# An fp32 network of two blocks on one core: two weight chunks behind each layer norm computed from the unnormalised residual, and new orders in the attentions

## The chip, the cores and the metric

One core of one Trainium2 chip. The metric is device time in microseconds (us); lower is better. Three runs of the kernel before gave a median of 1497.17 us (1496.08 to 1500.53).

## The reference, cut to what matters

The input is 256 tokens of width 1024, fp32. Two blocks follow one another, two layers each.

```
first block, per layer i:
  mix = s5_mixer(h) (i = 0)  or  stick_breaking_mixer(h) (i = 1: q, k, v = split(h @ w_qkv), 16 heads of 64)
  h = layer_norm(ALPHA * h + mix)                               # norm n = 0, then n = 2
  h = layer_norm(ALPHA * h + (silu(h @ w_g) * (h @ w_u)) @ w_down)   # n = 1, then n = 3
layer_norm(x) = (x - mean) * rsqrt(var + eps) * g + b
second block (the hybrid), per layer l:
  z = rmsnorm(x) @ w_in ;  split z into q_a k_a v_a | q_m k_m v_m o_m | gates
  x += (sigmoid(g_a) * (attention @ w_a) + sigmoid(g_m) * (mlstm @ w_m)) @ w_out
  x += relu(rmsnorm(x) @ w_ff1)**2 @ w_ff2
```

## The kernel before, in words

Activations lie transposed: features on 128 partitions, the T = 256 tokens on the free axis, in KT = 8 tiles (`kt`). Every weight matrix is cut into chunks of 128 x 2048 fp32 (1 MB) in the fixed order of `plan`. A chunk passes through one of RING = 3 slots: SyncE loads it into `raw` (L341 to L364, it waits for the subtraction of the chunk three before), ScalarE rounds it to `w_hi` (L369), VectorE makes `w_lo = raw - w_hi` (L374), TensorE multiplies. A product is three matmuls, hi x hi, hi x lo, lo x hi (L393 to L395), so a chunk is 48 matmuls of 128x128 on 256 columns. The split of the chunk three ahead is issued behind the work on the present chunk (`split_hi`, `split_lo`).

Each engine runs one program in order; the order is written by hand, and semaphores join the engines.

A sum that ends in a norm runs in `resid_tensor`, `resid_scalar`, `resid_vector`. VectorE adds each finished tile to `res`, forms `xn`, the residual less a rough mean, from tile 4 on, and TensorE turns sums and squares into the mean `dm` and the mean square (`layer_norm_tensor`, six fp32 matmuls, L689 to L694). Then `layer_norm_vector`: L907 to L912 make the variance, ScalarE makes `rstd` (L748, L751), and per tile VectorE scales (L890), ScalarE makes `x_hi` (L759; for n = 3 `res` at L754 and `x_hi` at L776), VectorE `x_lo` (L896 or L901); L915 subtracts the mean from two tiles at a time. `gemm_pair` (L403) then multiplies the first two chunks tile by tile as they come: gu0's chunks 0 and 1 behind n = 0, q0 and k0 behind n = 1, gu1's 0 and 1 behind n = 2, kv and qa0 behind n = 3. The SiLU table is loaded at L848 behind the norm.

First attention (`sb_tensor`, `sb_scalar`, `sb_vector`): twelve chunks in `SB_ORDER` and, for each of eight head pairs hp, `scores(hp)` (L997, needs the evicted k chunk, L540), `soft(hp)` on ScalarE (three passes, L1087 to L1093), `penalties(hp)` on VectorE (L1141, L1146), `running_sums(hp)` on TensorE (L1011), `weights(hp)` (L1099), `outputs(hp)` (L1023, needs the evicted v chunk). `chunk(name, 0)` and `(name, 1)` are the halves of a chunk.

Hybrid (`hyb_tensor`, `hyb_scalar`, `hyb_vector`): VectorE evicts each chunk times `rstd` (L2165). `squares_mean` and `last_square` feed `rstd`; `gate_products` (L1807), `keys`, `rows` and `queries` (L2191 to L2198) prepare; then for four pairs p: `scores(p)` (L1856), `maxima(p)`, `probabilities(p)` (ScalarE, L2053), `normalise(p)`, `transposed(p)` (TensorE), `turned(p)` (ScalarE, L2063), `outputs(p)` (L1881).

Of the kernel before, what the change touches and what calls it, by code (L numbers as in the profile page):

```python
# [24 lines left out]
P = 128  # L25
# [111 lines left out]
SB_ORDER = ("q0", "k0", "v0", "q1", "k1", "v1", "q2", "k2", "q3", "k3", "v2", "v3")  # L137
# [105 lines left out]
def stack(nc, w, out):  # L243
# [4 lines left out]
    with ctx:  # L248
# [30 lines left out]
        rstd = sb("rstd", [P, T], "rstd")  # L279
        vec_rows = sb("vec_rows", [108, P], "misc")  # L280
# [102 lines left out]
        def bank_of(g, k):  # L383
            if g.two:
                i = g.run0
                return (1, 2, 0)[i] if i < 3 else i % 2
            return (g.bank0 + k) % RING
# [15 lines left out]
        def gemm_pair(pe, one, two):  # L403

            items = (one, two)
            for g, idx in items:
                weights_split(pe, g.c0 + idx)
            for kt in range(KT):
                pe.wait_ge(xl_done, KT * one[0].x + kt + 1)
                for g, idx in items:  # L410
                    s = (g.c0 + idx) % RING
                    hi, lo = kt8_view(w_hi, s), kt8_view(w_lo, s)
                    for m in range(2):
                        last = three(PS[:, bank_of(g, idx), m * T:(m + 1) * T], hi[:, kt, m, :], lo[:, kt, m, :], x_hi[:, kt, :],
                                     x_lo[:, kt, :], kt == 0 and m == 0, kt == KT - 1)
                    if kt == KT - 1:
                        last.then_inc(chunk_done, 1)

        def gemm_tensor(pe, g, only=None, kts=(0, KT), first=0):
            drained, base = base_of(g)  # L420

            def body(idx, k, turn):
# [50 lines left out]
            chunk_loop(pe, g.n, max(gemm_head(g), first), 0, body, first)  # L473
# [49 lines left out]
        def gemm_scalar(act, g, only=None, part=None):  # L523
# [24 lines left out]
            chunk_loop(act, g.n, 0, 0, body)  # L548
# [15 lines left out]
        def gemm_vector(dve, g, only=None):  # L564
# [39 lines left out]
            chunk_loop(dve, g.n, 0, 0, body)  # L604
# [54 lines left out]
        
# [22 lines left out]
        def last_square(pe, n):
            pe.wait_ge(sq_done, 5 * n + 5)
            nc.tensor.matmul(PS[:, 5, 0:T], C("mean_d"), sqr[:, 1, T:2 * T], start=False, stop=True,
                             skip_group_check=True).then_inc(var_ready, 1)

        def layer_norm_tensor(pe, n):
            pe.wait_ge(centred, 3 * n + 3)
            nc.tensor.matmul(PS[:, 4, 0:T], C("mean_d"), prod[:, T:2 * T], start=True, stop=False, skip_group_check=True)  # L689
            pe.wait_ge(resid_done, KT * n + 7)  # L690
            nc.tensor.matmul(PS[:, 4, 0:T], C("mean_d"), xn[:, 6, :], start=False, stop=False, skip_group_check=True)
            squares_mean(pe, n)
            pe.wait_ge(resid_done, KT * n + 8)
            nc.tensor.matmul(PS[:, 4, 0:T], C("mean_d"), xn[:, 7, :], start=False, stop=True,  # L694
                             skip_group_check=True).then_inc(dm_ready, 1)
            last_square(pe, n)

        def resid_tensor(pe, g, n, first=True):
# [43 lines left out]
        def norm_scale(act, n):  # L742
# [5 lines left out]
            nc.scalar.activation(rstd[:, :], rstd[:, :] if n < 4 else PS[:, 5, 0:T], ACT.Ln, bias=eps).then_inc(act_step, 1)  # L748
# [4 lines left out]
        def normed_tile(act, n, kt):  # L753
            nc.scalar.activation(res[:, kt, :], xn[:, kt, :], ACT.Identity, bias=ln_bias(n, kt)).then_inc(res_normed, 1)  # L754

        def norm_hi(act, n):
            for kt in range(KT):
                act.wait_ge(scaled, KT * n + kt + 1)
                nc.scalar.activation(x_hi[:, kt, :], xn[:, kt, :], ACT.Identity, bias=ln_bias(n, kt)).then_inc(xh_done, 1)  # L759

        def fourth_norm_scalar(act):

            for kt in range(KT):
                act.wait_ge(scaled, KT * 3 + kt + 1)
                normed_tile(act, 3, kt)
                act.wait_ge(res_normed, KT * 3 + kt + 1)
                gained_hi(act, 4, kt)

        def fourth_squares(act):
            for q in range(3):  # L770
                square_pair(act, 4, None, q)
            square_tile(act, 4, None, 6)
            square_tile(act, 4, None, 7)

        def gained_hi(act, n, t):
            nc.scalar.activation(x_hi[:, t, :], res[:, t, :], ACT.Identity, scale=gain(n, t)).then_inc(xh_done, 1)  # L776

        def resid_scalar(act, g, n):
# [6 lines left out]
            if g.half:  # L785
# [14 lines left out]
                return  # L800
            if n < 4 and g.shape == "kt8":
                resid_hi(act, g, 0)
                nc.scalar.preload_act_table_set(LN_EXP)
                resid_hi(act, g, 1)
                square_pair(act, n, g, 0)
                square_pair(act, n, g, 1)
                square_pair(act, n, g, 2)
                resid_hi(act, g, 2)
                square_tile(act, n, g, 6)
            elif n < 4:  # L810
                for idx in range(7):
                    resid_hi(act, g, idx)
                nc.scalar.preload_act_table_set(LN_EXP)
                square_pair(act, n, g, 0)
                square_pair(act, n, g, 1)
                resid_hi(act, g, 7)
                square_pair(act, n, g, 2)
                resid_hi(act, g, 8)
                resid_hi(act, g, 9)
                square_tile(act, n, g, 6)  # L820
            elif n == 6:
# [11 lines left out]
                return  # L833
            else:
                for idx in range(g.n):
                    resid_hi(act, g, idx)
                return
            square_tile(act, n, g, 7)
            norm_scale(act, n)
            if n == 3:  # L840
                fourth_norm_scalar(act)
            else:
                norm_hi(act, n)
            resid_hi(act, g, last)
            if n == 3:
                fourth_squares(act)
            if n in (0, 2):
                nc.scalar.preload_act_table(ACT.Silu)  # L848
            if n < 3:
                for kt in range(KT):  # L850
                    normed_tile(act, n, kt)
# [28 lines left out]

        def add_squares(dve, n, i):
# [7 lines left out]
        def norm_scaled(dve, n, kt):  # L889
            nc.vector.scalar_tensor_tensor(out=xn[:, kt, :], in0=xn[:, kt, :], scalar=gain(n, kt),  # L890
                                           in1=rstd[:, :], op0=ALU.mult, op1=ALU.mult).then_inc(scaled, 1)

        def norm_lo(dve, n, kt):
            dve.wait_ge(scaled, KT * n + kt + 1)
            dve.wait_ge(xh_done, KT * x_index(n) + kt + 1)
            nc.vector.scalar_tensor_tensor(out=x_lo[:, kt, :], in0=xn[:, kt, :], scalar=ln_bias(n, kt),  # L896
                                           in1=x_hi[:, kt, :].bitcast(F32), op0=ALU.add, op1=ALU.subtract).then_inc(xl_done, 1)
# [6 lines left out]
        def layer_norm_vector(dve, n):  # L904
            dm = PS[:, 4, 0:T]
            dve.wait_ge(dm_ready, n + 1)
            nc.vector.tensor_copy(rstd[:, :], dm).then_inc(dve_step, 1)  # L907
            dve.wait_ge(dve_step, v_count.one())
            nc.vector.tensor_tensor(rstd[:, :], rstd[:, :], dm, ALU.mult).then_inc(dve_step, 1)
            dve.wait_ge(dve_step, v_count.one())  # L910
            dve.wait_ge(var_ready, n + 1)
            nc.vector.tensor_tensor(rstd[:, :], PS[:, 5, 0:T], rstd[:, :], ALU.subtract).then_inc(v_done, 1)  # L912

            def centre(q):
                nc.vector.tensor_tensor(xn[:, 2 * q:2 * q + 2, :], xn[:, 2 * q:2 * q + 2, :],  # L915
                                        dm.unsqueeze(1).to_broadcast([P, 2, T]), ALU.subtract).then_inc(dve_step, 1)
                dve.wait_ge(dve_step, v_count.one())

            centre(0)
            dve.wait_ge(rstd_done, n + 1)  # L920
            for kt in range(KT):
# [1605 lines left out]
```

## Time and profile before

| | |
|---|---|
| median of 3 runs | 1497.17 us |
| the profiled execution, its own time | 1498.88 us |
| its span in the trace | 1496.7 us |
| TensorE matmul busy | 1398.1 us, 93% |
| VectorE busy | 938.0 us, 63% |
| ScalarE busy | 676.1 us, 45% |
| mean granted TensorE clock | 0.978 of full |

PE is TensorE's matmuls, PEld its weight loads, DVE VectorE, ACT ScalarE, SP SyncE. A matmul's duration in the trace is longer than the distance to the next, since they overlap: rates are read from starts. Idle time stands in square brackets with what ended it.

### The profile page before, as it was taken

Reading aid. Unit: us, or ns where it says so; the run is one execution under the profiler, and the core shown is the slowest. Engines: PE = TensorE matmul, PEld = TensorE weight load, DVE = VectorE, ACT = ScalarE, POOL = GpSimd, SP = SyncE. Lnnn points to the kernel's source line nnn. Section 1 sums busy time; section 2 is a strip of 40 time slices with the busy share of each in tenths; the row PEclk is TensorE's granted clock in tenths of the full one; section 3 lists DMA queues with packets and bytes.
Section 4 is the critical chain, followed back from the end, with each engine's and each line's share of the span. In section 5 each row is a group of like instructions: output and inputs, shape, how many; then the busy total and the mean of one; then the engine's idle time right before and its main releaser. Section 6 shows DMA issues by size and latency. Waiting matters only on the chain.

```text
span 1496.7 us, 27718 instructions
## 1 busy us (share of the span) xinstructions
PE 1398.1 (93%) x11695; PEld 1354.5 (90%) x11695; DVE 938.0 (63%) x1217; ACT 676.1 (45%) x805; POOL 10.1 (1%) x8
## 2 busy tenths in 40 slices
PE   4859989999899989999898999999999899999998
PEld 4649989999889989999887999999999799999998
DVE  7996676555654575655675568776457566776542
ACT  4745453333464454343454444534344445444332
POOL 0100000000000000000000000000000000000000
PEclk9979999999999999999999999999999999999999
DMA  6087647676343447666343344556764335456661
GB/s 123 4 126 194 191 112 196 173 192 171 122 159 114 132 111 197 179 187 180 113 142 113 113 166 145 193 172 183 192 189 141 114 113 174 159 174 187 183 192 58
DMA packets 340445, 227.49 MB, mean 152 GB/s; under 512 B 21673, under 2 KB 335249, under 8 KB 340129
## 3 DMA queue, kind: packets, MB, share of 16 engines
q1 hardware_dynamic: 340352, 226.14, 52.9%
q8 instruction: 73, 1.20, 0.4%
q14 instruction: 20, 0.16, 0.0%
HBM read 222.70 MB, written 1.05 MB: 149 GB/s over the span
## 4 chain that ended last, share of the span: by engine, by line
PE 76%; DVE 9%; ACT 7%; issue 3%; SPq 3%; DMA 1%; ACTq 0%; DVEq 0%
PE PS L393 24%; PE PS L394 23%; PE PS L395 23%; ACT w_hi L369 4%; DVE w_lo L374 2%; SPq L1289 2%; PE PS L1011 1%; ACT a_prob L2053 1%; DMA x_chunk<-in_x_dram 1%; PE PS L1357 1%; ACT x_group L1454 0%; DMA raw<-in_ssm_w_glu_dram 0%; PE PS L1322 0%; DVE prod L645 0%; DVE hid_lo L649 0%
## 5 line engine op out<-in xcount | busy, mean ns | idle before, releaser
L374 DVE TENSOR_TENSOR w_lo<-raw,w_hi 128x2048 fp32r<-128x2048 f32 x208 | 476.4, 2291 | 242.7 <-ACT w_hi L369 232.9
L393 PE MATMUL PS<-x_hi,w_hi 128*128 128x256 f32 x1952 | 564.7, 289 | 20.5 <-DVE x_lo L896 11.6
L394 PE MATMUL PS<-x_lo,w_hi 128*128 128x256 f32 x1952 | 559.0, 286 | 0.0
L395 PE MATMUL PS<-x_hi,w_lo 128*128 128x256 f32 x1952 | 558.7, 286 | 0.0
L369 ACT ACTIVATE w_hi<-raw 128x2048 fp32r<-128x2048 f32 x208 | 396.6, 1907 | 243.9 <-PE PS L395 243.6
L393 PEld LDWEIGHTS PS<-x_hi,w_hi 128*128 128x128 f32 x1952 | 381.5, 195 | 25.7 <-issue 20.8
L394 PEld LDWEIGHTS PS<-x_lo,w_hi 128*128 128x128 f32 x1952 | 381.4, 195 | 0.1
L395 PEld LDWEIGHTS PS<-x_hi,w_lo 128*128 128x128 f32 x1952 | 381.4, 195 | 0.0
L393 PE MATMUL PS<-hid_hi,w_hi 128*128 128x256 f32 x1248 | 354.7, 284 | 6.6 <-DVE hid_lo L649 6.6
L394 PE MATMUL PS<-hid_lo,w_hi 128*128 128x256 f32 x1248 | 353.1, 283 | 0.0
L395 PE MATMUL PS<-hid_hi,w_lo 128*128 128x256 f32 x1248 | 353.1, 283 | 0.0
L393 PEld LDWEIGHTS PS<-hid_hi,w_hi 128*128 128x128 f32 x1248 | 239.5, 192 | 8.1 <-DVE hid_lo L649 7.4
L394 PEld LDWEIGHTS PS<-hid_lo,w_hi 128*128 128x128 f32 x1248 | 239.5, 192 | 0.1
L395 PEld LDWEIGHTS PS<-hid_hi,w_lo 128*128 128x128 f32 x1248 | 239.5, 192 | 0.0
L532 ACT ACTIVATE gate_sb<-PS 128x256 f32<-128x256 f32 x52 | 19.9, 383 | 164.2 <-PE PS L395 164.1
L574 DVE TENSOR_TENSOR prod<-PS,gate_sb 128x256 f32<-128x256 f32 x52 | 22.0, 424 | 80.9 <-ACT gate_sb L532 80.9
L535 ACT ACTIVATE gate_sb<-gate_sb 128x512 f32<-128x512 f32 x32 | 20.2, 632 | 99.4 <-DVE gate_sb L587 99.4
L618 DVE SCALAR_TENSOR_TENSOR res<-res,PS 128x256 f32<-128x256 f32 x48 | 19.9, 417 | 38.1 <-PE PS L395 37.9
L393 PE MATMUL PS<-w_hi,x_hi 128*128 128x256 f32 x128 | 37.3, 291 | 0.0
L2053 ACT ACTIVATE a_prob<-PS,neg_m,q_inv 128x128 f32<-128x128 f32 (+1 forms) x32 | 15.9, 506 | 46.3 <-DVE mx L2256 46.3
L901 DVE SCALAR_TENSOR_TENSOR x_lo<-res,vec,x_hi 128x256 fp32r<-128x256 f32 x32 | 15.5, 484 | 33.3 <-ACT x_hi L776 33.3
L394 PE MATMUL PS<-w_lo,x_hi 128*128 128x256 f32 x128 | 36.2, 282 | 0.0
(334 smaller groups left out, 1175.0 us busy)
## 6 DMA issues: line engine op xcount, KB each, us to landing
raw<-in_w_ff_dram SPq DMA_DIRECT2D x128, 512.0 KB, 4.6
raw<-in_ffn_w_gu_dram SPq DMA_DIRECT2D x88, 512.0 KB, 5.0
raw<-in_w_in_dram SPq DMA_DIRECT2D x68, 512.0 KB, 4.7
raw<-in_sb_w_qkv_dram SPq DMA_DIRECT2D x24, 512.0 KB, 4.4
raw<-in_ffn_w_down_dram SPq DMA_DIRECT2D x20, 512.0 KB, 5.0
raw<-in_ssm_w_glu_dram SPq DMA_DIRECT2D x16, 512.0 KB, 6.1
raw<-in_w_out_dram SPq DMA_DIRECT2D x16, 512.0 KB, 4.4
raw<-in_ssm_w_out_dram SPq DMA_DIRECT2D x8, 512.0 KB, 4.0
```

What stands on the lines that cost most here:

```text
L369: nc.scalar.activation(w_hi[s][:, :], raw[s][:, :], ACT.Copy).then_inc(hi_done, 1)
L374: nc.vector.tensor_tensor(w_lo[s][:, :], raw[s][:, :], w_hi[s][:, :].bitcast(F32), ALU.subtract).then_inc(lo_done, 1)
L393: nc.tensor.matmul(dst, lhs_hi, r_hi, start=start, stop=False, skip_group_check=True)
L394: nc.tensor.matmul(dst, lhs_hi, r_lo, start=False, stop=False, skip_group_check=True)
L395: return nc.tensor.matmul(dst, lhs_lo, r_hi, start=False, stop=stop, skip_group_check=True)
L532: nc.scalar.activation(gate_sb[:, k, 0:T], PS[:, bank, T:2 * T], g.func).then_inc(sig_done, 1)
L535: nc.scalar.activation(gate_sb[:, k, :], gate_sb[:, k, :], ACT.Square).then_inc(u_done, 1)
L574: nc.vector.tensor_tensor(prod[:, 0:T], PS[:, bank, 0:T], gate_sb[:, k, 0:T], ALU.mult).then_inc(z_done, 1)
L618: nc.vector.scalar_tensor_tensor(out=res[:, t, :], in0=res[:, t, :], scalar=g.alpha, in1=PS[:, tile_bank(g, t), 0:T], op0=ALU.mult, op1=AL ...
L901: nc.vector.scalar_tensor_tensor(out=x_lo[:, t, :], in0=res[:, t, :], scalar=gain(n, t), in1=x_hi[:, t, :].bitcast(F32), op0=ALU.mult, op1 ...
L1289: sp.dma_start(toep[SH * t:SH * t + SH, BQ * b:BQ * b + BQ, SH * t:P], kern[32 * b:32 * b + SH, :, 0:P - SH * t]).then_inc(k_moved, 16)
L2053: nc.scalar.activation(a_prob[p % 2][:, hd, cols], PS[:, 4 + hd, cols], ACT.Exp, bias=neg_m[:, p, hd, blk:blk + 1], scale=q_inv[:, p, hd, ...
```

## The change

Two chunks behind each of the four layer norms (n = 0 to 3) no longer wait for the normalised tiles. ScalarE and VectorE make `raw_hi` and `raw_lo` from `xn * g` while the sum still runs, with two further columns, -g and b, so that each such matmul moves 258 columns. The norm is applied behind the matmul: `early = (product + dm * colsum0) * rstd`, and then the bias, `colsum1`. The norm's own tiles are worked in pairs, the chunks' splits stand between them, and in the residual of shape kt8 (n = 0 and 2) two splits (`resid_lo` of the last two) move behind tile 7. The SiLU table load moves in front of the normed tiles. The third chunk (gu's number 2, q1, qa1) is now the first that waits for normalised tiles. Both attentions get other orders. Core of the diff:

```diff
-SB_ORDER = ("q0", "k0", "v0", "q1", "k1", "v1", "q2", "k2", "q3", "k3", "v2", "v3")
+SB_ORDER = ("q0", "k0", "q1", "k1", "v0", "q2", "k2", "v1", "q3", "k3", "v2", "v3")
+        def early_tensor(pe, n, slot, kts=(0, KT)):
+            for kt in range(*kts):
+                if slot == 0:
+                    pe.wait_ge(raw_lo_done, KT * n + kt + 1)
+                for m in range(2):
+                    last = three(early_banks(slot)[:, m, 0:T + 2], hi[:, kt, m, :], lo[:, kt, m, :], raw_hi[:, kt, :],
+                                 raw_lo[:, kt, :], kt == 0, kt == KT - 1)
# resid_tensor, behind the last block
             if n < 4:
+                early_tensor(pe, n, 0, (0, 4))
                 layer_norm_tensor(pe, n)
+                early_tensor(pe, n, 0, (4, KT))
+                early_tensor(pe, n, 1)
# ScalarE
+        def layer_norm_scalar(act, g, n):
+            resid_hi(act, g, g.n - 1)
+            norm_scale(act, n)
+            if n in (0, 2):
+                nc.scalar.preload_act_table(ACT.Silu)
+            normed_pair(act, n, 0)
+            normed_pair(act, n, 1)
+            early_columns(act, n, 0)      # two small copies of the column sums, then w_hi of the chunk three on
+            normed_pair(act, n, 2)
+            normed_pair(act, n, 3)
+            early_columns(act, n, 1)
+            early_scalar(act, n, 0)       # SiLU of the gate half, or two bias passes into q0 / k0 / kv / qa0
+            early_scalar(act, n, 1)
+        def normed_pair(act, n, q):       # res of two tiles, then x_hi of both
# VectorE, layer_norm_vector behind the variance (raw_tile_lo: one STT of 256 per tile, earlier, in resid_vector)
             centre(0)
             dve.wait_ge(rstd_done, n + 1)
+            scale(0); centre(1); scale(1); low(0); centre(2); scale(2); low(1)
+            split(0)                      # w_lo of the chunk three on
+            centre(3); scale(3); low(2); low(3)
+            split(1)
+            normalised(0)                 # two STT of 256 from PSUM, one product of 512
+            normalised(1)
+            if n in (0, 2): early_gated(dve, n, 0); early_gated(dve, n, 1)
# first attention, TensorE
-            gemm_pair(pe, (G["q0"], 0), (G["k0"], 0)) ; chunk("v0") ; scores(0) ; chunk("q1", 0) ; scores(1)
-            chunk("q1", 1) ; running_sums(0) ; chunk("k1", 0) ; running_sums(1) ; chunk("k1", 1) ; outputs(0)
...
+            chunk("q1") ; scores(0) ; chunk("k1", 0) ; scores(1) ; chunk("k1", 1) ; running_sums(0)
+            chunk("v0", 0) ; running_sums(1) ; chunk("v0", 1) ; outputs(0) ; scores(2) ; chunk("q2", 0)
+            outputs(1) ; scores(3) ; chunk("q2", 1) ; running_sums(2) ; chunk("k2", 0) ; running_sums(3)
+            chunk("k2", 1) ; scores(4) ; chunk("v1", 0) ; scores(5) ; chunk("v1", 1) ; outputs(2)
+            running_sums(4) ; chunk("q3", 0) ; outputs(3) ; running_sums(5) ; chunk("q3", 1) ; chunk("k3")
+            scores(6) ; chunk("v2", 0) ; scores(7) ; chunk("v2", 1) ; outputs(4) ; running_sums(6)
+            chunk("v3", 0) ; outputs(5) ; running_sums(7) ; chunk("v3", 1) ; outputs(6)
...
# first attention, ScalarE
+            chunk("q1") ; soft(0) ; chunk("k1") ; soft(1) ; weights(0) ; chunk("v0") ; weights(1) ; soft(2)
+            chunk("q2") ; soft(3) ; weights(2) ; chunk("k2") ; weights(3) ; soft(4) ; chunk("v1")
...
# hybrid, TensorE
+            if l: chunk("kv") ; squares_mean(pe, 6) ; last_square(pe, 6) ; chunk("qa0")
+            chunk("qa1") ; chunk("oa0")
+            if l == 0: squares_mean(pe, 4) ; last_square(pe, 4)
+            gate_products() ; chunk("oa1", 0)
+            # l = 1: keys, gate_rows, chunk("oa1", 1); l = 0: chunk("oa1", 1), keys, gate_rows
# hybrid, ScalarE
+            if l == 0: fourth_squares(act) ; split("qa1") ; norm_scale(act, 4) ; key_squares()
...
-            split("qm") ; probabilities(1) ; split("km") ; turned(0) ; probabilities(2) ; split("vm0") ; turned(1)
+            split("qm") ; split("km") ; turned(0) ; probabilities(1) ; split("vm0") ; turned(1) ; probabilities(2)
# hybrid, VectorE, l = 0
+                square_sums(dve, 4) ; lo("qa1") ; wait rstd_done, early_set ; rescale("kv") ; rescale("qa0")
+                evict("qa1") ; evict("oa0") ; gate_parts() ; keys() ; lo("oa0")
             rows() ; queries(0) ; evict("oa1") ; queries(1)      # as before; l = 1 moves gate_parts and keys behind lo("oa0")
```

## Rows read from the trace of the kernel before

**Rows 1.** Page, part 4: the chain that ended last, share of the span by engine.
```profile
PE 76%; DVE 9%; ACT 7%; issue 3%; SPq 3%; DMA 1%; ACTq 0%; DVEq 0%
```

**Rows 2.** Waits of PE: us in total, times, longest us.
```profile
PE PS L1881 <- ACT a_probT L2063: 11.8, 6, 2.4
PE PS L393 <- DVE x_lo L896: 11.6, 3, 3.9
...
PE PS L393 <- DVE x_lo L901: 4.3, 1, 4.3
...
PE PS L1023 <- DVE hid_lo L1153: 1.0, 1, 1.0
```

**Rows 3.** Windows: us, busy us (count) by engine, PEclk, DMA share, GB/s.
```profile
240.00:350.00 110.00, 110.00 (x919) 110.00 (x918) 62.62 (x69) 40.73 (x35) 0.00 (x0) 1.00 0.67 182
...
202.00:204.00 2.00, 2.00 (x13) 2.00 (x12) 1.97 (x5) 0.99 (x2) 0.00 (x0) 0.57 0.00 0
...
813.00:814.00 1.00, 1.00 (x12) 0.68 (x14) 1.00 (x1) 0.00 (x0) 0.00 (x0) 1.00 0.00 0
...
825.00:826.00 1.00, 1.00 (x7) 1.00 (x6) 0.93 (x5) 0.99 (x3) 0.00 (x0) 0.50 0.00 0
```

**Rows 4.** Timeline of PE, norm n = 3 and hybrid: start us, us, line.
```profile
729.29 0.59 PE L689 MATMUL PS<-prod,const 128*128 128x256 f32 x2
...
761.08 0.55 PE L393 MATMUL PS<-x_hi,w_hi 128*128 128x256 f32 x1 [3.46 <-DVE w_lo L374]
...
785.31 0.37 PE L1856 MATMUL PS<-qk_rot 64*128 64x128 f32 x1
...
812.90 0.65 PE L1881 MATMUL PS<-a_probT,va_tok 128*64 128x256 f32 x4 [2.41 <-ACT a_probT L2063]
...
823.86 0.65 PE L1881 MATMUL PS<-a_probT,va_tok 128*64 128x256 f32 x4 [2.40 <-ACT a_probT L2063]
```

**Rows 5.** Timeline of PE: first mean of n = 0 and n = 1, first scores.
```profile
189.53 0.59 PE L689 MATMUL PS<-prod,const 128*128 128x256 f32 x2
...
193.40 0.59 PE L684 MATMUL PS<-sqr,const 128*128 128x256 f32 x2
...
391.36 0.59 PE L689 MATMUL PS<-prod,const 128*128 128x256 f32 x2
...
416.92 0.70 PE L997 MATMUL PS<-qkv 64*128 64x256 f32 x4
```

**Rows 6.** Timeline of DVE around norm n = 0.
```profile
188.88 2.29 DVE L374 TENSOR_TENSOR w_lo<-raw,w_hi 128x2048 fp32r<-128x2048 f32 x1 [0.65 <-ACT w_hi L369]
...
197.64 0.68 DVE L915 TENSOR_TENSOR xn<-xn,PS 128x512 f32<-128x512 f32 x1
198.35 0.48 DVE L890 SCALAR_TENSOR_TENSOR xn<-xn,vec,rstd 128x256 f32<-128x256 f32 x1
```

**Rows 7.** Timeline of ACT behind norm n = 0.
```profile
206.61 1.28 ACT L848 ACT_TABLE_LOAD   x1
207.90 3.31 ACT L754 ACTIVATE res<-xn,vec 128x256 f32<-128x256 f32 x8
...
223.75 0.38 ACT L532 ACTIVATE gate_sb<-PS 128x256 f32<-128x256 f32 x1 [3.57 <-PE PS L395]
```

**Rows 8.** Page, part 6: DMA issues, count, KB each, us to landing.
```profile
raw<-in_ffn_w_gu_dram SPq DMA_DIRECT2D x88, 512.0 KB, 5.0
```

**Rows 9.** Timeline of ACT, first attention: an eviction, one pass of `soft`.
```profile
453.94 0.60 ACT L540 ACTIVATE qkv<-PS 128x512 f32<-128x512 f32 x1 [2.12 <-PE PS L395]
...
474.54 0.85 ACT L1090 ACTIVATE sb_soft<-sb_soft 128x768 f32<-128x768 f32 x1
```

**Rows 10.** Timeline of DVE, first attention: first half of `penalties`.
```profile
421.91 0.96 DVE L1141 SCALAR_TENSOR_TENSOR sb_nl<-PS,sb_soft 128x768 f32<-128x768 f32 x1 [0.16 <-ACT sb_soft L1093]
```

**Rows 11.** Timeline of PE, first attention: `running_sums(1)` after its wait.
```profile
431.23 1.03 PE L1011 MATMUL PS<-sb_nl,const 128*128 128x256 f32 x5 [1.45 <-DVE sb_nl L1146]
```

**Rows 12.** Timeline of ACT, hybrid: the pass that `outputs(1)` waits for.
```profile
812.04 0.81 ACT L2063 ACTIVATE a_probT<-PS 128x768 f32<-128x768 f32 x1
```

More of the change, by code:

```diff
@@ L401, in kt8_view, with early_banks @@
             return w[s][:, :].rearrange("p (k m n) -> p k m n", k=8, m=2)
[L403 to L417 removed]
+        def early_banks(slot):
+            return PS[:, 4 + 2 * slot:6 + 2 * slot, :]
+        def early_tensor(pe, n, slot, kts=(0, KT)):
+            g, idx = early_chunks(n)[slot]
+            s = (g.c0 + idx) % RING
+            if kts[0] == 0:
+                weights_split(pe, g.c0 + idx)
+            hi, lo = kt8_view(w_hi, s), kt8_view(w_lo, s)
+            for kt in range(*kts):
+                if slot == 0:
+                    pe.wait_ge(raw_lo_done, KT * n + kt + 1)
+                    if kt == 0:
+                        pe.wait_ge(col_lo_done, 2 * n + 2)
+                for m in range(2):
+                    last = three(early_banks(slot)[:, m, 0:T + 2], hi[:, kt, m, :], lo[:, kt, m, :], raw_hi[:, kt, :],
+                                 raw_lo[:, kt, :], kt == 0, kt == KT - 1)
+            if kts[1] == KT:
+                last.then_inc(chunk_done, 1)
         def gemm_tensor(pe, g, only=None, kts=(0, KT), first=0):
             drained, base = base_of(g)
+            begun_early = g.func is ACT.Silu or g.name in SB_ORDER
             def body(idx, k, turn):
@@ new lines, in early_scalar @@
+        def early_scalar(act, n, slot):
+            g, idx = early_chunks(n)[slot]
+            act.wait_ge(early_done, 2 * n + slot + 1)
+            act.wait_ge(cols_copied, 2 * n + slot + 1)
+            bias = [col_sums[:, 2 * slot + m, 1:2] for m in range(2)]
+            if g.evac == "gated":
+                gate = early[:, slot, T:2 * T]
+                nc.scalar.activation(gate, gate, g.func, bias=bias[1]).then_inc(sig_done, 1)
+                return
+            dst = hyb_tiles(g) if n == 3 else proj(g, 0).rearrange("p (a t) -> p a t", a=2)
+            for m in range(2):
+                ins = nc.scalar.activation(dst[:, m, :], early[:, slot, m * T:(m + 1) * T], ACT.Identity, bias=bias[m],
+                                           scale=g.scale)
+            ins.then_inc(early_set if n == 3 else act_done, 1)
@@ L836, in resid_scalar, with fourth_squares @@
                     resid_hi(act, g, idx)
[L837 to L851, printed above, removed]
+        def fourth_squares(act):
+            for q in range(3):
+                square_pair(act, 4, None, q)
+            square_tile(act, 4, None, 6)
+            square_tile(act, 4, None, 7)
         def shift_sum(dve, n):
@@ L887, in add_squares, with square_sums @@
             dve.wait_ge(sq_added, 3 * n + i + 1)
[L889 to L897, printed above, removed]
+        def square_sums(dve, n, first=0, end=3):
+            for i in range(first, end):
+                add_squares(dve, n, i)
         def gained_lo(dve, n, t):
@@ new lines, in split, with normalised @@
+            def split(slot):
+                e, idx = early_chunks(n)[slot]
+                split_lo(dve, e.c0 + RING, idx, idx)
+            def normalised(slot):
+                e, idx = early_chunks(n)[slot]
+                dve.wait_ge(cols_copied, 2 * n + slot + 1)
+                for m in range(2):
+                    ins = nc.vector.scalar_tensor_tensor(out=early[:, slot, m * T:(m + 1) * T], in0=dm_sb[:, :],
+                                                         scalar=col_sums[:, 2 * slot + m, 0:1],
+                                                         in1=early_banks(slot)[:, m, 0:T], op0=ALU.mult, op1=ALU.add)
+                ins.then_inc(dve_step, 1)
+                dve.wait_ge(dve_step, v_count.one())
+                both = early[:, slot, :].rearrange("p (a t) -> p a t", a=2)
+                nc.vector.tensor_tensor(both, both, twice[1], ALU.mult).then_inc(early_done, 1)
@@ L919, in layer_norm_vector @@
             centre(0)
             dve.wait_ge(rstd_done, n + 1)
-            for kt in range(KT):
-                norm_scaled(dve, n, kt)
-                if n < 3 and kt >= 1:
-                    norm_lo(dve, n, kt - 1)
-                elif kt >= 1:
-                    gained_lo(dve, 4, kt - 1)
-                if kt % 2 and kt < 7:
-                    centre(kt // 2 + 1)
-            if n < 3:
-                norm_lo(dve, n, 7)
-            else:
-                gained_lo(dve, 4, 7)
-        def square_sums(dve, n, first=0, end=3):
-            for i in range(first, end):
-                add_squares(dve, n, i)
+            scale(0)
@@ L938, in resid_vector @@
         def resid_vector(dve, g, n):
             last = g.n - 1
+            held = 2 if g.shape == "kt8" and n < 4 else last
             for idx in range(g.n):
@@ L958, in resid_vector @@
                     if t == 5 and n < 8:
-                        square_sums(dve, n, 0, 1 if g.half else 3)
-                    if t == 7 and g.half:
+                        square_sums(dve, n, 0, 1 if g.half or n < 4 else 3)
+                    if t == 6 and n < 4 or t == 7 and g.half:
                         square_sums(dve, n, 1, 3)
-                if idx < last or n >= 4:
+                if n >= 4 or idx < held:
                     resid_lo(dve, g, idx)
             if n < 4:
-                layer_norm_vector(dve, n)
-                resid_lo(dve, g, last)
-            if n == 3:
-                square_sums(dve, 4)
+                for idx in range(held, g.n):
+                    resid_lo(dve, g, idx)
+                layer_norm_vector(dve, g, n)
         qkv = sb("qkv", [P, 16, T], "hh", 16 * 4 * T)
@@ L2131, in hyb_scalar @@
             nc.scalar.preload_act_table_set(LN_EXP)
-            split("g0")
-            turned(3)
             split("g1")
```

435 lines of the change are left out of this document (275 added, 160 removed).

## The prediction

> **What bounds the kernel now.** I read the chain by engine first: TensorE holds 76% of it [rows 1], against 93% busy in the table ahead, so time is TensorE's stream plus its gaps. Then the list of what TensorE waits for: 15.9 us in front of the first product behind the four layer norms (L393 on `x_lo`) and 11.8 us in front of the hybrid's `outputs` (L1881 on ScalarE's copy) [rows 2]. Then windows, for the rate: in a stretch of plain products 919 matmuls take 110 us, 0.12 us each, so a chunk of 48 is 5.8 us [rows 3]. The windows also show the second price of a gap. Behind it the granted clock is 0.5, 1.2 GHz: a matmul then takes 0.21 us, and it was still at 0.57 in 202 to 204 us, where the products had begun again at 197.9. One such stretch costs 1.4 to 2.4 us (3.3 to 5.6 us long, 15 to 26 matmuls by 0.09). Which gap brings it is not settled by its length: 2.41 us of idle (812.90) left the clock at 1.00, 2.40 us (823.86) were followed by 0.50 [rows 3, 4]. So I price a gap of 2 to 3 us at half a drop, a longer one at a whole drop.
>
> **Method.** For each region I kept a ledger in the new order: an instruction starts when its engine is free and its releaser has ended, with durations from rows. Its zero is the first mean (L689) of the norm in the trace [rows 4, 5]. Times below are from there.
>
> **FFN entries, n = 0 and 2.** TensorE: 24 early matmuls 2.9, six means to 5.5 (L689 is two records in 0.59 with the last one's tail, 0.43 from mean to mean [rows 5]), 24 and 48 early ones to 14.3. These need no normalised tile, so the old idle stretch is gone. What is late next is gu's chunk 2, the first that needs `x_lo`. VectorE [rows 6]: tile 7 and two `raw_lo` (0.48 each) to 2.4, the two held `w_lo` (2.29 each) to 6.8, three variance steps to 8.1; ScalarE's two for `rstd` to 9.1. Then the table load, 1.28 [rows 7], now in the path: 10.4. A pair costs ScalarE 1.5 (two passes of 0.41 pitch and latency 0.1, one of 512 columns 0.6), VectorE 2.0 (three of 0.68). Pairs 0 and 1 are ready at 12.7 and 14.6, in time. Then ScalarE makes a `w_hi` (1.9) and VectorE its `w_lo` (2.3) before pairs 2 and 3, ready at 19.8 and 21.5. TensorE has done half of chunk 2 at 17.2, idles 2.6, later 0.3, and ends chunk 3 at 29.0. In the trace ScalarE sees chunk 3 at 223.75 - 189.53 = 34.2 [rows 5, 7]. That is -5.2; a gap of 2.6 us may drop the clock, 1.2 on average: -4.0 each, -8.0 for both (-5 to -10.4). The two `w_lo` behind tile 7 free their `raw` slots some 6 us later on SyncE's queue; a load lands in 5.0 us [rows 8], by 12, and its `w_hi` starts at 13.6 at the earliest. Nothing else waits in that queue.
>
> At this place a rule speaks against the change. Row: the load starts 0.02 us behind the pass in front and the next pass starts at 207.90, 1.29 us on [rows 7]; no further pause shows. The Trainium skill, ScalarE: Activation LUTs, What ACT_TABLE_LOAD costs, says a switch costs a drain besides, about 2.66 us in all. By that each FFN entry would lose 1.4 us more, by the row nothing. I go by the row.
>
> **First attention, n = 1.** One `w_lo` less and no table load: pairs 2 and 3 at 18.3 and 20.1, q1 multiplied by 21.6 (idle 1.1 and 0.3). The next order is `scores(0)`, which needs k0 evicted. k0's product is ready at 14.3, but VectorE gets to it only behind pair 3 and the `w_lo` of v0 (23.7): two `normalised` of 1.5 to 26.7, ScalarE's bias passes to 27.6. TensorE idles 6.1 us, queued behind it k1, which is ready; `scores(0)` starts at 27.7. Before: 416.92 - 391.36 = 25.6 [rows 5], also with three chunks done. So +2.1, and +1.9 for the clock behind a gap of 6.1.
>
> The new order then puts six users right behind the last half of the chunk they need (outputs(0), (2), (4), (6) on v, scores(4), (6) on k). Each waits for the chunk's eviction: 0.2 to notice, 0.60 for the pass [rows 9], 0.07 on: 0.87, together +5.2. `running_sums(3)` comes 5.1 us behind q2's end, while `soft(3)` now stands behind q2's eviction and split: 0.2 + 0.5 + 1.8 + three passes of 0.85 + 1.65 of `penalties` (L1141, and L1146 with 0.69) = 6.7 [rows 9, 10]: +1.6. `running_sums(1)` has that wait already, 1.45 [rows 11], and gets 0.2 more; `outputs(1)` and `(7)` wait 0.3 and 1.1 for the pair before, and the old 1.0 at L1023 goes [rows 2]. Sum +7.4. Two waits of 1.7 at half a drop of 0.8: +0.8. First attention: 2.1 + 1.9 + 7.4 + 0.8 = +12.2.
>
> **Hybrid, layer 0.** qa1 and oa0 are done at 28.0. The mean of squares now needs five squares of a ScalarE that finished the bias passes at 28.4, and three sums of VectorE: 32.5, idle 4.5 and a drop. `rstd` comes behind a `w_hi` on ScalarE, at 36.0. The old idle of 3.46 at 761.08 [rows 4], also behind `rstd`, goes; it is in the 56.0 below. From there on VectorE is the chain: `w_lo` 37.0, four evictions 39.5, key rotation to 47.3 (waiting for ScalarE's key scale), `w_lo` 49.5, `rows` 52.8, two query rotations of 2.6 with one eviction: `scores(0)` at 58.6. The same ledger over the old order gives 55.1, the trace 785.31 - 729.29 = 56.0, so I take 59.5: +3.5. It follows an idle of 5.3: a drop, +1.5.
> Then the gain: `turned(p)` no longer stands behind `probabilities(p+1)` on ScalarE. It ends 12.6 behind `scores(0)`, `outputs(0)` is due at 14.7. The waits of 1.85, 2.41 and 2.40 go, with the drop behind the third: -8.1. Layer 0: -3.1.
>
> **Hybrid, layer 1.** `gate_products` comes a chunk later, so `scores(0)` waits for the rotations, 1.0. The other three waits of L1881 (11.8 - 6.7 = 5.1 [rows 2]) go, and one drop of 1.5: -5.6.
>
> **Added and unseen.** 384 early matmuls move 258 columns, 0.8% more, 0.3 us; no row shows any width but 256 in this form (bounds below). The column copies and two small products are 0.3 us off the path. DMA traffic is the same.
>
> **Sum** against the profiled execution's 1498.88 (span 1496.7): -8.0 + 12.2 - 3.1 - 5.6 + 0.3 = -4.2, 1494.7. That execution is 1.7 over the median; from the median, **1493.0**.
>
> **Rivals.**
> 1. *The norms' gaps close and the attention absorbs the rest*: `scores(0)` is not stalled for long and evictions don't show. For it: VectorE is 63% busy. Against: both k0's eviction and the pairs stand in one queue with three `w_lo`. Without the 7.4 and half of the 4.0: 1493 - 9.4 = 1483.6. Chance 0.14.
> 2. *Slower: the wait moves instead of going.* In the hybrid, `scores(p+1)` needs `probabilities(p)`. `probabilities(1)` now stands behind `turned(0)`, and my ledger leaves only 0.8 us between its end and `scores(2)`. If ScalarE's chain is over 0.8 us longer than I count, the wait comes back there; if it comes back whole, 13.2 of gain (-8.1 and -5.1) is lost: 1506. It turns the sign from 4.2 of that on. For it: that queue already made the old wait (L2063 starts right at the end of a w_hi [rows 12]). Against: the pieces moved are each measured. Chance 0.14.
> 3. *258 columns are not at 256's rate.* Speaking for it: no row. Against: nothing in the rate of rows 3 depends on the last columns. At half rate 384 x 0.09 = +36: 1529; no change at 0.011 us a matmul. Chance 0.04.
> 4. *The change is even*: every 2.6 us gap drops the clock and the short attention waits do too, +4: 1497. Chance 0.22.
> The forecast keeps 0.46, its own range 1489 to 1496.
>
> **Numbers.** Under 0.3% (4.5 us) this kernel can't be told from no change. Faster by more, under 1492.7: rival 1 and near half of the forecast and a part of rival 4, 0.42. Within: 0.38. Slower, over 1501.7: rivals 2 and 3 and tails, 0.20. The range takes in rival 1 in part and rival 4: 1484 to 1503.
>
> **What would show it.** Right: no idle stretch over 1 us between the residual's end and the third chunk; 2 to 3 us inside chunk 2 of gu; L997 first starting some 27 to 28 us behind the norm's first mean with an idle of 5 to 7 us; six idles near 0.9 us in front of `outputs` and `scores`; no idle in front of `outputs` in the hybrid, and idles of 4 to 5 us at the first mean of squares and at `scores(0)` of hybrid layer 0. Wrong: `scores(0)` of the first attention with under 3 us idle (then rival 1), idles in front of the second hybrid `scores` (rival 2), early matmuls more than 0.13 us apart (rival 3).

## The result, and the profile after

The changed kernel takes 1504.74 us (median of 4 runs, 1502.73 to 1507.06) against 1496.62: ratio 1.005, 95% interval 1.0027 to 1.0074. It is 8.1 us slower, where 4.2 less were forecast.

The chain by engine (page, part 4) gives less to TensorE and more to the two others than in [rows 1]:

```profile
PE 73%; DVE 12%; ACT 10%; issue 3%; SPq 2%; DMA 1%; ACTq 0%; DVEq 0%
```

The waits of TensorE after (us in total, times, longest), to be held against [rows 2]. The wait at the hybrid's `outputs` is gone, as forecast. The first of these rows has nothing of before and nothing in the prediction to answer to it:

```profile
PE PS L705 <- DVE prod L942: 8.8, 2, 4.4
...
PE PS L400 <- DVE x_lo L1025: 7.0, 4, 2.4
...
PE PS L1990 <- DVE qk_rot L2343: 6.3, 2, 5.3
PE PS L1142 <- ACT qkv L847: 5.7, 1, 5.7
...
PE PS L712 <- DVE sqr L988: 3.6, 1, 3.6
PE PS L1156 <- DVE sb_nl L1286: 3.4, 2, 1.7
```

I cut the span at the first mean of each norm. It is L689 before [rows 4, 5] and L723 after; of its starts I take off 2.9 us, since 24 early matmuls now stand in front of it. The two further cuts are the waits of 1.8 us near the end of each hybrid layer (L1920 before, L2054 after, on `hid_lo`). Timeline of TensorE after: the missed wait, the four means, and the waits that were forecast:

```profile
181.64 0.80 PE L705 MATMUL PS<-prod,const 128*128 128x256 f32 x1 [4.39 <-DVE prod L942]
...
196.79 0.60 PE L723 MATMUL PS<-prod,const 128*128 128x256 f32 x2
...
213.40 0.39 PE L400 MATMUL PS<-x_hi,w_hi 128*128 128x256 f32 x1 [2.39 <-DVE x_lo L1025]
...
394.43 0.60 PE L723 MATMUL PS<-prod,const 128*128 128x256 f32 x2
...
419.98 1.22 PE L1142 MATMUL PS<-qkv 64*128 64x256 f32 x4 [5.71 <-ACT qkv L847]
...
549.34 0.60 PE L723 MATMUL PS<-prod,const 128*128 128x256 f32 x2
...
746.83 0.60 PE L723 MATMUL PS<-prod,const 128*128 128x256 f32 x2
...
777.12 0.86 PE L712 MATMUL PS<-sqr,const 128*128 128x256 f32 x2 [3.58 <-DVE sqr L988]
...
803.06 0.58 PE L1990 MATMUL PS<-qk_rot 64*128 64x128 f32 x1 [5.29 <-DVE qk_rot L2343]
```

| stretch, us | before | after | difference | forecast |
|---|---|---|---|---|
| start to the first mean of n = 0 | 189.53 | 193.89 | +4.4 | 0 |
| n = 0 to n = 1 (FFN) | 201.83 | 197.64 | -4.2 | -4.0 |
| n = 1 to n = 2 (first attention and its residual) | 136.11 | 154.91 | +18.8 | +12.2 |
| n = 2 to n = 3 (FFN) | 201.82 | 197.49 | -4.3 | -4.0 |
| n = 3 to the end of hybrid layer 0 | 147.35 | 142.92 | -4.4 | -3.1 |
| to the end of hybrid layer 1 | 371.59 | 365.57 | -6.0 | -5.6 |
| rest | 248.47 | 248.48 | 0 | 0 |

The sum is +4.2, from two single executions; the first row holds 2.6 us of luck in the start-up (TensorE's first GLU matmul at 115.84 against 118.41). From there to the first mean it is 78.05 against 71.12: +6.9. So two rows are off, by 6.9 and 6.6, and each holds one wait at L705.

**What L705 waits for.** It is `shift_mean`, the rough mean of the first four tiles. VectorE's timeline after:

```profile
169.01 0.78 DVE L633 SCALAR_TENSOR_TENSOR res<-res,PS 128x256 f32<-128x256 f32 x2 [0.89 <-PE PS L402]
177.28 0.18 DVE L972 SCALAR_TENSOR_TENSOR raw_lo<-vec,raw_hi 128x8 fp32r<-128x8 f32 x1 [7.49 <-ACT raw_hi L802]
177.37 0.17 DVE L974 TENSOR_TENSOR raw_lo<-vec,raw_hi 128x8 fp32r<-128x8 f32 x1
177.45 2.28 DVE L381 TENSOR_TENSOR w_lo<-raw,w_hi 128x2048 fp32r<-128x2048 f32 x1
179.65 0.74 DVE L633 SCALAR_TENSOR_TENSOR res<-res,PS 128x256 f32<-128x256 f32 x2
180.43 0.69 DVE L940 TENSOR_TENSOR prod<-res 128x512 f32<-128x512 f32 x1
181.16 0.43 DVE L942 TENSOR_TENSOR prod<-prod 128x256 f32<-128x256 f32 x1
```

and ScalarE's, same stretch:

```profile
169.37 1.91 ACT L376 ACTIVATE w_hi<-raw 128x2048 fp32r<-128x2048 f32 x1 [3.58 <-PE PS L402]
171.30 1.28 ACT L893 ACT_TABLE_LOAD   x1
175.13 1.91 ACT L376 ACTIVATE w_hi<-raw 128x2048 fp32r<-128x2048 f32 x1 [2.54 <-PE PS L402]
176.95 0.20 ACT L801 ACTIVATE raw_hi<-vec 128x8 fp32r<-128x8 f32 x1
177.05 0.20 ACT L802 ACTIVATE raw_hi<-vec 128x8 fp32r<-128x8 f32 x1
```

The reader is to see a chain through three queues (a split is numbered here by the chunk of the residual whose slot it takes over). VectorE reaches the low parts of the two further columns (0.18 and 0.17 us) behind tile 1, in chunk 0 of the residual. ScalarE makes their high parts behind `w_hi` number 1, which waits until TensorE has finished chunk 1. VectorE idles 7.49 us, and `w_lo` number 0, tiles 2 and 3 and the sum for L705, none of which needs the columns, stand behind. Before, that `w_lo` waited for nothing but its own `w_hi`, and the sum ended at 179.38, in time for TensorE. VectorE's timeline of the kernel before:

```profile
173.96 2.29 DVE L374 TENSOR_TENSOR w_lo<-raw,w_hi 128x2048 fp32r<-128x2048 f32 x1 [1.52 <-ACT w_hi L369]
...
178.96 0.42 DVE L858 TENSOR_TENSOR prod<-prod 128x256 f32<-128x256 f32 x1
```

In the FFN's residual (n = 1 and 3) the sum runs over ten chunks, the columns come in time and L705 doesn't wait. Behind the 4.39 us TensorE ran at 1.2 GHz (the first of the windows below; the second is behind the 2.39 us, the third is `k1` behind `scores(0)`; columns as in [rows 3], the granted clock behind the five engines):

```profile
182.00:184.00 2.00, 2.00 (x9) 1.82 (x9) 2.00 (x2) 0.00 (x0) 0.00 (x0) 0.50 1.15 324
216.00:218.00 2.00, 2.00 (x13) 2.00 (x12) 1.45 (x1) 0.52 (x1) 0.00 (x0) 0.57 0.24 59
422.00:424.00 2.00, 2.00 (x11) 2.00 (x11) 0.00 (x0) 1.94 (x4) 0.00 (x0) 0.50 0.00 0
```

### The profile page after: what moved, and what is told of

It is laid out like the page before. It is cut to its first block, busy times and chain, and to the rows that moved or that the text cites. A ratio compares the mean times of both kernels' runs of the same rounds, so it can differ in the third digit from the quotient of the medians.

```text
span 1500.9 us, 27760 instructions
## 1 busy us (share of the span) xinstructions
PE 1396.3 (93%) x11695; PEld 1353.0 (90%) x11695; DVE 956.1 (64%) x1255; ACT 689.2 (46%) x853; POOL 10.1 (1%) x8
## 4 chain that ended last, share of the span: by engine, by line
PE 73%; DVE 12%; ACT 10%; issue 3%; SPq 2%; DMA 1%; ACTq 0%; DVEq 0%
PE PS L400 22%; PE PS L401 22%; PE PS L402 22%; DVE w_lo L381 4%; ACT w_hi L376 4%; SPq L1423 1%; PE PS L1156 1%; PE PS L1475 1%; DMA x_chunk<-in_x_dram 1%; ACT res L815 1%; PE PS L1491 1%; ACT terms L1617 1%; DMA raw<-in_ssm_w_glu_dram 0%; ACT x_group L1588 0%; PE PS L1456 0%
## 5 line engine op out<-in xcount | busy, mean ns | idle before, releaser
L400 PE MATMUL PS<-x_hi,w_hi 128*128 128x256 f32 x1824 | 524.6, 288 | 11.3 <-DVE x_lo L1025 7.0
L401 PE MATMUL PS<-x_lo,w_hi 128*128 128x256 f32 x1824 | 519.4, 285 | 0.0
L402 PE MATMUL PS<-x_hi,w_lo 128*128 128x256 f32 x1824 | 519.2, 285 | 0.0
L400 PEld LDWEIGHTS PS<-x_hi,w_hi 128*128 128x128 f32 x1824 | 353.3, 194 | 16.1 <-DVE x_lo L1025 7.8
L401 PEld LDWEIGHTS PS<-x_lo,w_hi 128*128 128x128 f32 x1824 | 353.4, 194 | 0.1
L402 PEld LDWEIGHTS PS<-x_hi,w_lo 128*128 128x128 f32 x1824 | 353.2, 194 | 0.0
L400 PE MATMUL PS<-raw_hi,w_hi 128*128 128x258 f32 x128 | 36.9, 288 | 0.0
L402 PE MATMUL PS<-w_hi,x_lo 128*128 128x256 f32 x128 | 36.1, 282 | 0.0
```

The source lines that it names most:

```text
L400: nc.tensor.matmul(dst, lhs_hi, r_hi, start=start, stop=False, skip_group_check=True)
L401: nc.tensor.matmul(dst, lhs_hi, r_lo, start=False, stop=False, skip_group_check=True)
L402: return nc.tensor.matmul(dst, lhs_lo, r_hi, start=False, stop=stop, skip_group_check=True)
```

## The experiments

All ratios are to the kernel before, run beside them (1496.38 for the first four, 1496.08 for the others).

**e1, the columns earlier.**

```diff
                 for idx in range(begin + 1):
                     resid_hi(act, g, idx)
+                    if idx == (0 if g.shape == "kt8" else 1):
+                        raw_columns_hi(act, g, n)
                     if idx == 0:
                         nc.scalar.preload_act_table_set(LN_EXP)
-                    if idx == 1:
-                        raw_columns_hi(act, g, n)
```

> The changed kernel with one pair of small passes moved: in the residuals of n = 0 and 2 ScalarE makes the two high columns (L801, L802) behind the w_hi of chunk 0 and ahead of the table load, no longer behind the w_hi of chunk 1. Theory (the missed wait): VectorE stood 7.49 us at its low columns for them, and that made TensorE's shift_mean (L705) wait 4.4 us twice, each with a stretch at the low clock of 1.3 to 2.5 us behind it. Without it 2 x (4.4 + 2.0) = 12.8 less than the changed kernel's 1504.7: 1492, and no wait at L705. Rival A: shift_sum is late anyway, since a w_lo and two tiles stand in front of it; then L705 still waits 2 us or more and the time stays at 1498 or above. Rival B: most of the 8 us lies in the first attention, which took 18.8 us more against 12.2 of my ledger; then only about 6 come back, 1498.

Measured: 1492.85, ratio 0.9976 (0.9966 to 0.9987): 11.9 us less than the changed kernel. VectorE's sum is ready in time, and L705 is gone from the list of waits:

```profile
172.73 0.18 DVE L972 SCALAR_TENSOR_TENSOR raw_lo<-vec,raw_hi 128x8 fp32r<-128x8 f32 x1 [1.73 <-ACT raw_hi L802]
172.82 0.17 DVE L974 TENSOR_TENSOR raw_lo<-vec,raw_hi 128x8 fp32r<-128x8 f32 x1
172.91 2.29 DVE L381 TENSOR_TENSOR w_lo<-raw,w_hi 128x2048 fp32r<-128x2048 f32 x1
...
177.53 0.42 DVE L942 TENSOR_TENSOR prod<-prod 128x256 f32<-128x256 f32 x1
```

TensorE's timeline of e1 starts L705 without idle:

```profile
178.30 0.59 PE L705 MATMUL PS<-prod,const 128*128 128x256 f32 x2
```

From the first GLU matmul (117.05) to the first mean it is 71.01 us, as before the change (71.12). n = 1 to n = 2 takes 148.26. Both rivals fall: neither does a wait stay at L705, nor is the first attention's excess over my ledger its own. This one misplaced pair of 0.2 us passes made the change slower; with it mended the change is 3.5 us faster than before (0.24%).

**e2, ScalarE's hybrid order alone, on the kernel before.**

```diff
             split("qm")
-            probabilities(1)
             split("km")
             turned(0)
-            probabilities(2)
+            probabilities(1)
             split("vm0")
             turned(1)
-            probabilities(3)
+            probabilities(2)
             split("vm1")
             turned(2)
+            probabilities(3)
```

> The kernel before with one thing alone: on ScalarE turned(p) goes ahead of probabilities(p+1) in both hybrid layers. Theory: the six waits at outputs (11.8 us) go, with two low-clock stretches of 1.5 behind them (three of the waits were long enough): 1496.6 - 13 = 1483.5, and scores(p+1) doesn't wait. Rival (rival 2 of the prediction): the wait comes back at scores(p+1), which needs probabilities(p); then the waits sum to over 8 us again and the time is over 1491.

Measured: 1483.06, ratio 0.9909 (0.9894 to 0.9925): -13.3. The head of its list of waits, nothing left out; a row for L1881 would stand second, with 11.8:

```profile
PE PS L1394 <- DMA toep<-kern: 11.8, 1, 11.8
PE PS L393 <- DVE x_lo L896: 11.6, 3, 3.9
PE PS L1296 <- DMA tb<-in_ssm_log_dt_dram: 8.0, 1, 8.0
PE PS L393 <- DVE hid_lo L649: 6.6, 4, 1.7
PE PS L1302 <- DMA c_rows<-in_ssm_c_re_dram: 4.5, 1, 4.5
PE PS L393 <- DVE x_lo L901: 4.3, 1, 4.3
```

Layer 0 is 7.0 shorter in the trace, layer 1 6.9. So the part of the change that is worth most is three calls moved in one engine's list, and rival 2 is refuted: `scores(p+1)` doesn't take the wait over. One term is not as the prediction had it. The stretch at the low clock behind layer 0's third wait (0.50 in 825 to 826 us before) was counted among the gains. In this execution the wait is gone and the granted clock is 0.54 in 826 to 828 us all the same, with no idle in front of it.

**e3, e1 with other orders in the first attention.** Chunks in the changed kernel's sequence; TensorE's list begins

```diff
             chunk("q1")
-            scores(0)
             chunk("k1", 0)
-            scores(1)
             chunk("k1", 1)
-            running_sums(0)
+            scores(0)
             chunk("v0", 0)
-            running_sums(1)
             chunk("v0", 1)
-            outputs(0)
-            scores(2)
+            scores(1)
+            running_sums(0)
             chunk("q2", 0)
...
```

and ScalarE's and VectorE's lists follow it; in the same manner each user stands half a chunk or more behind what it needs.

> e1_columns with other orders in the first attention on the three engines: the same chunks in the same sequence, but scores, running sums and outputs stand at least half a chunk behind the eviction and the passes that they need, and scores(0) stands behind k1. Theory (order): the 15 us of waits in this attention and the drop behind the 5.7 us one come from where the users stand; the ledger gives 121.3 us for the stretch against 139.7, so 18.4 less than e1_columns: 1473.5. Rival (work): VectorE and ScalarE are the limit there, and the waits only move; then under 6 us come back, over 1486.

Measured: 1474.05, ratio 0.9860 (0.9845 to 0.9875): 18.8 less than e1. n = 1 to n = 2 takes 129.83, and from `scores(0)` on TensorE has no idle over 0.3 us in the attention. The engines were not the limit; the order was.

**e5, only TensorE's list, and only behind `k1`.**

```diff
             chunk("k1", 1)
-            running_sums(0)
             chunk("v0", 0)
-            running_sums(1)
             chunk("v0", 1)
+            running_sums(0)
+            running_sums(1)
             outputs(0)
             scores(2)
             chunk("q2", 0)
...
```

> e1_columns with only TensorE's list in the first attention changed, and that only behind k1: scores, running sums and outputs 1 to 7 stand half a chunk or more behind the eviction or pass that they need. scores(0), scores(1) and the lists of ScalarE and VectorE are those of the changed kernel. It splits the first attention's price in two. Theory: the eight short waits there (0.7 to 1.7 us each, my +7.4 and +0.8) are the place of the users alone; the ledger gives 129.1 against 139.7, so 10.6 less than e1_columns: 1482.3. What is left to e3_attention (1474.05), 8.2, is the wait of scores(0) for k0's late eviction and the low clock behind it. Rival: with ScalarE and VectorE unchanged the waits only move along TensorE's list; then 1488 or more.

Measured: 1482.08, ratio 0.9904 (0.9887 to 0.9921): 10.8 less than e1. The one idle over 0.3 us left between `scores(0)` and the residual's end is that of `scores(0)` itself:

```profile
413.61 1.23 PE L1142 MATMUL PS<-qkv 64*128 64x256 f32 x4 [4.82 <-ACT qkv L847]
```

So of 18.8 us, 10.8 were users put right behind an eviction or a pass. The other 8.0 (1482.08 - 1474.05) I put down to the entry: `scores(0)` behind VectorE's queue, 4.82, and the low clock behind it (0.50 in 414 to 418 us). That is argued, since e3 also reorders the lists of ScalarE and VectorE; but e5 has no other wait over 0.3 us behind q1 that e3 could remove.

**e4, e3 with other orders behind the norms.**

```diff
# ScalarE
+            early_columns(act, n, 0)
+            normed_pair(act, n, 0) ; (1) ; (2) ; (3)
             if n in (0, 2):
                 nc.scalar.preload_act_table(ACT.Silu)
-            normed_pair(act, n, 0) ; (1) ; early_columns(act, n, 0) ; normed_pair(act, n, 2) ; (3)
             early_columns(act, n, 1)
# VectorE (the last held resid_lo stood ahead of the variance)
-            centre(0) ; rstd ; scale(0) ; centre(1) ; scale(1) ; low(0) ; centre(2) ; scale(2) ; low(1) ; split(0)
-            centre(3) ; scale(3) ; low(2) ; low(3) ; split(1) ; normalised(0) ; normalised(1)
+            centre(0) ; (1) ; (2) ; rstd ; scale(0) ; (1) ; resid_lo(last) ; scale(2) ; low(0) ; centre(3) ; scale(3)
+            low(1) ; (2) ; (3) ; split(0) ; normalised(0) ; normalised(1) ; split(1)
```

> e3_attention with other orders behind the four norms: all four pairs of normed tiles before the second w_hi and before both w_lo of the next chunks, the last held w_lo behind rstd instead of ahead of the variance, the table load behind the pairs, the early chunks' eviction ahead of the second w_lo. Theory: the idle of 2.4 us inside the third chunk and the low clock behind it (1.5) go at n = 0, 2 and 3, and the mean of squares and the first scores of hybrid layer 0 come 3.8 earlier: 2 x 4.3 + 1.6 + 3.8 = 14 less than e3_attention. Rival: the w_lo that is put back is late for the fourth chunk and the idle moves there; then under 5 us less.

Measured: 1463.24, ratio 0.9777 (0.9763 to 0.9791): -10.8 against e3, of the 14 expected. Per stretch the traces show -3.9 and -4.0 at the FFN entries (198.26 to 194.41, 198.07 to 194.09), -2.0 in the attention and -2.2 in hybrid layer 0. The idle inside the third chunk is gone; what is left there is 0.38 and 0.70 us for the fourth chunk's `w_lo`, the rival in small. The first scores of layer 0 start 54.6 us behind the norm's first mean, where e3 has 59.1: 4.5 earlier, for the 3.8 expected. Behind them this execution has two stretches at 1.2 GHz (granted clock 0.54 in 806 to 808 us, 0.50 in 820 to 822), where e3's stands at 1.00, and so only 2.2 of the 4.5 are left at the layer's end. In layer 1, which wasn't touched, it has 3.0 more, in two such stretches again.

**e6, e4 with hybrid layer 0's statistics pulled forward.**

```diff
# ScalarE, n = 3, behind the four pairs (was behind the bias passes of kv and qa0)
+                for q in range(3): square_pair(act, 4, None, q)
+                square_tile(act, 4, None, 6) ; square_tile(act, 4, None, 7)     # behind early_columns(1)
# ScalarE, hybrid: norm_scale(4), which makes rstd, ahead of split("qa1")
# VectorE: square_sums(4) behind split(0); in the hybrid lo("qa1"), lo("oa0") ahead of keys()
# TensorE, layer 0
-            chunk("oa0") ; squares_mean(4) ; last_square(4) ; gate_products() ; chunk("oa1") ; keys() ; gate_rows()
+            chunk("oa0", 0) ; squares_mean(4) ; last_square(4) ; chunk("oa0", 1) ; gate_products()
+            chunk("oa1", 0) ; keys() ; gate_rows() ; chunk("oa1", 1)
```

> e4_norm with hybrid layer 0 changed: ScalarE squares the normed tiles right behind them, ahead of the bias passes of kv and qa0, TensorE takes the mean of squares in the middle of oa0, and rstd comes some 8 us earlier; the key scale and two w_lo are pulled forward with it. Theory: the 2.1 us wait at the mean of squares and 3 of the 5 us at scores(0) were rstd's lateness; the ledger has scores(0) at 49.1 instead of 54.3 behind the norm's first mean: 5.2 less than e4_norm, 1458.0. Rival: VectorE's rotations and rows set scores(0) whatever rstd does; then only the 2.1 come back, 1461.

Measured: 1455.18, ratio 0.9724 (0.9702 to 0.9746): -8.1 against e4, where 5.2 were expected; the traces of both give -5.8 in layer 0 (140.99 to 135.19). In e4 the two waits were 2.06 and 5.01, with one of 1.94 at `row_columns` between them, which e6 no longer has. Timelines of e4, `rstd` and the first scores:

```profile
737.92 0.42 ACT L790 ACTIVATE rstd<-rstd 128x256 f32<-128x256 f32 x1
...
760.91 0.58 PE L1992 MATMUL PS<-qk_rot 64*128 64x128 f32 x1 [5.01 <-DVE qk_rot L2345]
```

and of e6, the mean of squares besides:

```profile
731.53 0.70 PE L712 MATMUL PS<-sqr,const 128*128 128x256 f32 x2 [1.08 <-DVE early L1049]
...
734.65 0.42 ACT L790 ACTIVATE rstd<-rstd 128x256 f32<-128x256 f32 x1
...
755.68 0.58 PE L2000 MATMUL PS<-qk_rot 64*128 64x128 f32 x1 [3.09 <-DVE qk_rot L2350]
```

From the norm's first mean, `scores(0)` starts at 49.4 instead of 54.6, as the ledger had it (49.1 for 54.3). But `rstd` ends only 3.2 earlier than in e4 (28.8 for 32.0); the expectation's 8 us is right only against the changed kernel (36.7). So `rstd` accounts for at most 3.2 of the 5.2, and the rest came with VectorE's order and the place of `keys` and `gate_rows`, which the edit moves too; the parts were not tried alone. The rotations keep 3.1 of wait.

**e7, e6 with `scores(0)` of layer 0 behind the first half of `km`.**

```diff
-            scores(0)
+            if l: scores(0)
             chunk("km", 0)
+            if l == 0: scores(0)
             chunk("km", 1)
```

> e6_squares with scores(0) of hybrid layer 0 half a chunk later, behind the first half of km. Theory: the ledger leaves 3.6 us of wait in front of scores(0); half a chunk is 2.9 us, so 0.7 stays, the low clock behind it (2 us) goes, and scores(1), now 3 us behind scores(0), waits 1.3 for probabilities(0): 1.7 + 2.0 = 3.7 less, 1454.3. Rival: the wait moves whole to scores(1), the clock drops there; then within 1 us of e6_squares.

Measured: 1455.45, ratio 0.9729 (0.9710 to 0.9748), the same as e6. The traced execution has layer 0 at 132.21, 3.0 less, with the wait moved to `scores(1)`:

```profile
759.91 0.37 PE L2000 MATMUL PS<-qk_rot 64*128 64x128 f32 x1 [2.42 <-ACT a_prob L2201]
```

The medians don't bear the 3.0 out. By them the rival holds, the trace leans to the theory, and with either interval about 3 us wide to each side this stays open.

e6 and e7 are the fastest. e6 is 41 us (2.8%) under before and 49.6 under the changed kernel, with the same arithmetic as the latter.

## Why the prediction was wrong

**The step that failed** is this sentence: "The column copies and two small products are 0.3 us off the path." It is the only one in which the passes for the two further columns can be counted, and it puts them off the path. Their size was about right (0.20, 0.20, 0.18 and 0.17 us, overlapping). I didn't ask what VectorE's two wait for, nor what is queued behind them. That cost 6.9 us at n = 0 and 6.65 at n = 2 (154.91 - 148.26): 13.5 in all, the wait of 4.39 and a stretch at the low clock each time. With it the sum is -4.2 + 13.5 = +9.3, against 8.1 measured. Without it, e1 took 1492.85, and the prediction says 1493.0. That they agree so well is in part luck: from the first mean to the end e1's trace is 5.9 shorter than before, where the ledger has 4.2. The ledger couldn't show it, since its zero was the first mean: what the change adds to the residual lies ahead of that zero, and was costed by hand.

**FFN entries, -4.0 each: right** (-4.2, -4.3). The idle inside chunk 2 was 2.39 us for 2.6, and the clock fell behind both, where I had reckoned with half. At n = 0 some sixteen matmuls then came 0.21 apart instead of 0.12, about 1.5 us; with that in place of the 1.2 the ledger would have said -3.7.

The table load in the path was 1.28 us, and the next pass began 1.29 behind its start, as in [rows 7]:

```profile
202.35 1.28 ACT L855 ACT_TABLE_LOAD   x1
203.64 0.60 ACT L815 ACTIVATE res<-xn,vec 128x256 f32<-128x256 f32 x1
```

The Trainium skill, ScalarE: Activation LUTs, What ACT_TABLE_LOAD costs, has a drain besides, 2.66 us in all. This trace doesn't show one, and the row was the better guide.

**First attention, +12.2: right in size, in part because its errors cancel.** With the L705 wait taken away (e1) the stretch is 148.26 - 136.11 = +12.15. `scores(0)` started at 28.4 (419.98 - 394.43 + 2.9) for 27.7, after 5.71 idle for 6.1. The six waits for an eviction took 0.69 to 0.78 each for 0.87, 4.4 for 5.2 in all, and both `running_sums` waits 1.71. The 0.8 for a low clock behind those two was not spent: the granted clock is 1.00 from 427 to 535 us. Behind `scores(0)` it was low for longer than the 1.9 allows, from 419 to 426 us. e5 and e3 show that all of it was order: moving the users alone gives 10.8 back.

**Hybrid: right in sum, loose in its parts.** Layer 0 -4.4 for -3.1, with waits of 3.58 and 5.29 for 4.5 and 5.3, and `scores(0)` at 59.1 for 59.5; layer 1 -6.0 for -5.6. The gain at `outputs` came nearly whole: -13.3 alone in e2, where the prediction's terms make -14.7 (8.1, 5.1 and the 1.5 of layer 1; rival 2 adds them up without the last).

**258 columns: no cost.** From 199.19 to 213.40 TensorE did 96 matmuls, 72 of them early ones, in 14.21 less 2.39 of idle: 0.12 us each, the rate of [rows 3]. Rival 3 is out (its 36 is a slip: 384 x 0.09 is 34.6). A window of early matmuls:

```profile
200.00:210.00 10.00, 10.00 (x86) 10.00 (x85) 7.31 (x13) 8.39 (x14) 0.00 (x0) 1.00 0.79 199
```

The rival of the other sign was placed in the wrong spot, the hybrid's `scores`, where e2 shows nothing. The slower case came from a stretch that no rival named.

## What to carry to other kernels

An added instruction on an in-order engine is priced by what it waits for and by what stands behind it, not by its length: here 0.4 us of small passes cost 13.5. Begin the ledger at the first instruction that the diff adds, not where the gain is expected. And, in a kernel like this one, put every user half a chunk behind its producer's eviction: a wait of 0.7 us at each of six places, two of 1.7 and one late entry were 18.8 us, all got back by reordering three lists.

## What the runs showed of the hardware

The granted clock doesn't follow the length of an idle alone. Behind 2.39 us (n = 0 and 2 after) it fell to 0.5; behind 2.42 us (`scores(1)` in e7) it stayed at 1.00. Behind 1.88 us inside q1 it stayed at 1.00 in the changed kernel and fell to 0.5 in e1 and e5. And it falls with no idle at all. In e6 TensorE came to the end of a chunk at 810.77 and then worked through the mLSTM's `decays`, with no idle before any of these matmuls in the timeline; in the midst of them it went to half speed (windows of e6; 14 or so of the first window's 22 matmuls are those of `decays`):

```profile
810.00:813.00 3.00, 3.00 (x22) 2.29 (x20) 1.55 (x3) 1.34 (x3) 0.00 (x0) 1.00 0.00 0
813.00:816.00 3.00, 3.00 (x15) 2.62 (x16) 1.79 (x2) 1.35 (x4) 0.00 (x0) 0.51 0.11 11
```

Such stretches stood in one execution and not in another of the same list there (e4 and e3, in both hybrid layers), and are a part of why single traces differ by 3 us. What decides it was not tried.
